# Moving the norm and rotation of attention heads onto VectorE alone and turning them two products later, in PSUM banks of their own

## The reference, cut to what matters

```python
q = apply_rope(rms_norm(q.reshape(B, S, 2 * H, D), q_gain), cos, sin)   # D = 64, 2 * H = 16
def rms_norm(x, gain):
    y = xf * lax.rsqrt(jnp.mean(xf * xf, axis=-1, keepdims=True) + EPS)
    return y * gain
def apply_rope(x, cos, sin):
    return concatenate([x1 * c - x2 * s, x2 * c + x1 * s], axis=-1)
```

## Time and profile before

| what | value |
|---|---|
| median of 3 runs | 2499.97 us (2494.35 to 2503.65) |
| profiled execution, its own time | 2496.57 us |
| its span | 2494.7 us |
| granted clock of TensorE, mean | 0.96 |
| busy: PE, PEld, DVE, ACT, POOL | 91%, 77%, 61%, 48%, 13% |

### The profile page before, as it was taken

One profiled execution on the slowest core, in us unless ns is written; L12 is line 12 of the kernel. 1 busy time (PEld: TensorE's weight loads), 2 busy tenths in 40 slices (PEclk: granted clock), 3 DMA queues, 4 the chain that ended last, 5 costly groups with the idle time before them and its releaser, 6 DMA issues.

```text
span 2494.7 us, 29578 instructions
## 1 busy us (share of the span) xinstructions
PE 2279.3 (91%) x11690; PEld 1917.5 (77%) x11690; DVE 1525.2 (61%) x2036; ACT 1203.5 (48%) x1829; POOL 313.7 (13%) x238
## 2 busy tenths in 40 slices
PE   6999999787998899999999999859999777899999
PEld 6877888776887668888877887738887566688887
DVE  5645656576656366557636666676655776554655
ACT  4555545446444445445555445444445344444543
POOL 0001000631000001000002000211000433154000
PEclk9999999899999999999999999969999898989999
DMA  6535565213564315565545655405565444401563
GB/s 215 184 132 163 185 200 167 78 51 121 190 199 148 114 68 180 194 194 169 169 135 160 205 185 165 157 17 150 184 202 170 119 136 121 152 1 52 172 199 118
DMA packets 200504, 369.32 MB, mean 148 GB/s; under 512 B 6863, under 2 KB 142415, under 8 KB 200368
## 3 DMA queue, kind: packets, MB, share of 16 engines
q1 hardware_dynamic: 196752, 358.70, 44.3%
q0 software_dynamic: 3616, 8.74, 1.9%
HBM read 366.36 MB, written 1.05 MB: 147 GB/s over the span
## 4 chain that ended last, share of the span: by engine, by line
PE 82%; DVE 11%; ACT 5%; issue 2%; DMA 1%; SPq 0%; DVEq 0%; POOL 0%; ACTq 0%
PE PS L641 42%; PE PS L758 13%; PE PS L755 6%; PE PS L742 5%; DVE wlo L1729 2%; PE PS L911 2%; PE PS L775 2%; PE PS L1192 1%; PE PS L776 1%; DVE U L1752 1%; ACT whi L1248 1%; PE PS L1160 1%; PE PS L833 1%; PE PS L1061 1%; ACT U L1268 1%
## 5 line engine op out<-in xcount | busy, mean ns | idle before, releaser
L1729 DVE TENSOR_TENSOR wlo<-raw,whi 128x1024 fp32r<-128x1024 f32 x658 | 808.5, 1252 | 265.7 <-ACT whi L1248 264.8
L1248 ACT ACTIVATE whi<-raw 128x1024 fp32r<-128x1024 f32 x680 | 700.2, 1056 | 364.8 <-PE PS L641 309.9
L641 PE MATMUL PS<-whi,U 128*128 128x512 f32 x1792 | 505.3, 399 | 23.6 <-DVE U L1752 7.5
L758 PE MATMUL PS<-U,whi 128*128 128x512 f32 x1440 | 507.4, 397 | 0.0
L641 PEld LDWEIGHTS PS<-whi,U 128*128 128x128 f32 x1792 | 338.7, 191 | 100.7 <-issue 26.5
L755 PE MATMUL PS<-U,wlo 128*128 128x256 f32 x1260 | 353.5, 281 | 0.0
L758 PEld LDWEIGHTS PS<-U,whi 128*128 128x128 f32 x1440 | 264.4, 188 | 51.9
L641 PE MATMUL PS<-wlo,U 128*128 128x512 f32 x896 | 279.8, 394 | 0.0
L641 PE MATMUL PS<-whi,fH 128*128 128x512 f32 x832 | 258.2, 391 | 0.9 <-DVE fL L1977 0.9
L1854 DVE TENSOR_TENSOR AR<-PS,AR 128x512 f32<-128x512 f32 x96 | 66.4, 691 | 314.3 <-ACT AR L1331 314.3
L641 PE MATMUL PS<-wlo,fH 128*128 128x512 f32 x832 | 256.3, 389 | 0.0
(11 more groups left out here) (298 smaller groups left out, 2615.6 us busy)
## 6 DMA issues: line engine op xcount, KB each, us to landing
raw<-in_mlp_w_up SPq DMA_DIRECT2D x64, 1024.0 KB, 5.5
raw<-in_mlp_w_down SPq DMA_DIRECT2D x64, 1024.0 KB, 5.0
raw<-in_ret_w_in SPq DMA_DIRECT2D x48, 1024.0 KB, 5.2
raw<-in_m_w_up SPq DMA_DIRECT2D x32, 1024.0 KB, 5.5
raw<-in_m_w_down SPq DMA_DIRECT2D x32, 1024.0 KB, 4.9
raw<-in_kv_w SPq DMA_DIRECT2D x24, 1024.0 KB, 5.2
raw<-in_ret_w_out SPq DMA_DIRECT2D x16, 1024.0 KB, 4.9
raw<-in_gla_w_in SPq DMA_DIRECT2D x12, 1024.0 KB, 5.1
```

Of the source, the lines that this page charges most:

```text
L641: mm = e.matmul(bank(b + nb), a, w[:, nb * 512:(nb + 1) * 512], start=(begins and n < 2), stop=(ends and n >= 4))
L758: mm = e.matmul(o, w_h[:, k, :], U[:, k, :, :, :], start=(k == 0), stop=(k == 7))
L1248: e.activation(split_half(whi, i, x), a, ACT.Copy).then_inc(HI.tick((i, x)), 1)
L1729: e.tensor_tensor(split_half(wlo, i, x), a, split_half(whi, i, x).bitcast(F32), ALU.subtract).then_inc(LO.tick((i, x)), 1)
```

## The change

1. DVE does the whole norm and rotation, upper and lower rows, in one function `head_work`. Its eight weight splits for one product (2 halves of 4 chunks) are placed between its pieces. POOL keeps only the DMAs of the gains.
2. ACT copies both halves of a product out of PSUM as soon as it is done (`head_read`), and squares the copy in SBUF later (`head_squares`). `qs` and `xs` are doubled; the second ones lie in parts of `v` that are not written yet.
3. All products of DIL and DIFF use banks 0 to 3. Product n + 1 waits for HCP (or LV, the copy of a v product) of product n. All products after the first of a stage also take the quarters of tt = 0 first in their first chunk.
4. Heads are turned into banks 4 to 7. In DIL the heads of product m are turned inside product m + 2, after its first chunk (after the second for m = 1). In DIFF the first heads are turned after the second chunk of product 2, and the second heads after product 2, as before.
5. The rows for "kv" are turned inside product 2 after its third chunk. ACT and DVE write the first half of them to `U` at the end of product 2 and the other half at the start of product 3.
6. In the attention part of DIL the scores stand in banks 4 to 6, the turned probabilities in 0 to 2, the values in 3 and 7. The first scores no longer wait for the last v copies (LV).

```diff
@@ PE
-            def turn_heads(key, qs, banks, free):
+            def turn_heads(key, qs, free):
...
-                                e.wait_ge(*(HPOOL[key] if tt == 0 else HDVE[key]))
+                                e.wait_ge(*HROT[key + (tt,)])
...
             def pe_diff(S):
-                gemm_a((S, 1), c0 + 4, 8, u_ap, (4, 6))
-                k0, k1 = (S, 0), (S, 1)
-                turn_heads(k0, p.qs[0], (0, 1, 2, 3), [[HSQ[k0 + (0,)]], [], [HSQ[k0 + (1,)]], []])
-                gemm_a((S, 2), c0 + 8, 8, u_ap, (0, 2), free=([HTC[k0 + (1,)]], [HTC[k0 + (3,)]]))
-                turn_heads(k1, p.qs[1], (4, 5, 6, 7), [[HSQ[k1 + (0,)]], [], [HSQ[k1 + (1,)]], []])
+                gemm_a((S, 1), c0 + 4, 8, u_ap, (0, 2), free=([HCP[k0 + (0,)]], [HCP[k0 + (1,)]]), entry=lambda: None)
+
+                def v_product(c):
+                    if c == 1:
+                        turn_heads(k0, p.qs[0], [[]] * 4)
+
+                gemm_a((S, 2), c0 + 8, 8, u_ap, (0, 2), free=([HCP[k1 + (0,)]], [HCP[k1 + (1,)]]), after=v_product,
+                       entry=lambda: None)
+                turn_heads(k1, p.qs[1], [[HTC[k0 + (j,)]] for j in range(4)])
...
             def pe_dil(S):
+                def beside(n, c):
+
+                    m = n - 2
+                    if 0 <= m < 6 and c == (1 if m == 1 else 0):
...
+                        turn_heads((S, m), p.qs[m % 2], free)
+                    if (n, c) == (2, 2):
+                        turn_kv()
 
                 for n in range(9):
...
-                    gemm_a((S, n), c0 + 4 * n, 8, u_ap, bs, fresh=fresh_u(t) if n in (0, 3) else None, free=free_for(n),
-                           entry={0: lambda: turn_in(S, 1), 3: lambda: None}.get(n))
-                    if 1 <= n <= 6:
-                        o = bs_of[(n - 1) % 2]
-                        f0, f1 = read_out(n - 1)
-                        turn_heads((S, n - 1), p.qs, (o[0], o[0] + 1, o[1], o[1] + 1), [f0, [], f1, []])
+                    gemm_a((S, n), c0 + 4 * n, 8, u_ap, (0, 2), fresh=fresh_u(t) if n in (0, 3) else None,
+                           free=read_out(n - 1) if n else ((), ()), after=lambda c: beside(n, c),
+                           entry=(lambda: None) if n else (lambda: turn_in(S, 1)))
@@ ACT
             def act_dil(S):
...
                     if n:
                         hi_of(c0 + 4 * n, 1)
+                        if n == 3:
+                            e.wait_ge(*USED[c0 + 11, 1])
+                            for tt in range(2):
+                                u_hi((S, "kv"), tt, 1, IN_KV)
                         if m < 6:
...
+                            head_squares((S, m), p.qs[m % 2], p.xs[m % 2])
+                        hi_of(c0 + 4 * n + 1, 1)
+                        if m < 6:
                             root((S, m), st[:, 64:96])
...
+                        if 2 <= n < 8:
+                            turn_heads((S, n - 2), p.qT[n - 2] if n < 5 else p.kT[n - 5])
+                        hi_of(c0 + 4 * n + 2, 2)
+                        if n == 2:
+                            e.wait_ge(*USED[c0 + 9, 1])
+                            for tt in range(2):
+                                u_hi((S, "kv"), tt, 0, IN_KV)
+                    if n < 6:
+                        head_read((S, n), p.qs[n % 2])
@@ DVE
+            def head_work(key, qs, xs, tab, i):
+
+                lo_of(i, 1)
+                if key == (DIL, 2):
+                    for tt in range(2):
+                        u_lo_in((DIL, "kv"), tt, 1, IN_KV)
+                head_sum(key, 0, xs)
+                head_sum(key, 1, xs)
+                head_mean(key)
+                lo_of(i + 1, 1)
+                head_root(key)
+                head_scale(qs, 0)
+                head_scale(qs, 1)
+                head_swap(qs, xs, tab, 0)
+                lo_of(i + 2, 1)
+                head_swap(qs, xs, tab, 1)
+                head_sum_of_both(key, qs, xs, tab, 0)
+                lo_of(i + 3, 1)
+                head_sum_of_both(key, qs, xs, tab, 1)
@@ POOL
-                for n in range(6):
-                    head_rotate((S, n), p.qs, p.xs, p.tab)
-                    if n < 5:
-                        e.wait_ge(*HTAB[S, n])
+                for n in range(5):
+                    e.wait_ge(*HTAB[S, n])
...
```

More of the change, by code:

```diff
@@ L258, in program @@
                 turns.append((S, "kv"))
-        turned = [(t, tt, j) for t in turns for tt in range(2) for j in range(2)]
+        turned = []
+        for t in turns:
+            turned += [(t, tt, j) for tt in range(2) for j in range(2)] if t[1] != "kv" else \
+                      [(t, tt, j) for j in range(2) for tt in range(2)]
         TURN = Event(sem("s_u_turned"), turned)
@@ new lines, in turn_kv @@
+                def turn_kv():
+                    e.wait_ge(*HTC[S, 0, 3])
+                    for j in range(2):
+                        for tt in range(2):
+                            turn_quarter((S, "kv"), tt, j, h)
+                def beside(n, c):
+                    m = n - 2
+                    if 0 <= m < 6 and c == (1 if m == 1 else 0):
+                        if m == 0:
+                            free = [[]] * 4
+                        elif m == 1:
+                            free = [[UL[(S, "kv"), j // 2, j % 2]] for j in range(4)]
+                        else:
+                            free = [[HTC[S, m - 1, j]] for j in range(4)]
+                        turn_heads((S, m), p.qs[m % 2], free)
+                    if (n, c) == (2, 2):
+                        turn_kv()
@@ L1260, in prime, with u_hi @@
                 e.activation(st[:, 200:201], ones[:, 0:1], ACT.Sqrt)
[L1262 to L1269, removed]
+            def u_hi(t, tt, j, gain):
+                e.wait_ge(*TURN[t, tt, j])
+                for kk in range(4):
+                    k, o = 4 * j + kk, (4 + 2 * tt + j) * 512 + kk * 128
+                    ins = e.activation(U[:, k, tt, 0, :], PS[:, o:o + 128], ACT.Copy, scale=gT[:, gain, k:k + 1])
+                ins.then_inc(UH.tick((t, tt, j)), 1)
             def u_hi_o(S):
@@ L1279, in next_in @@
             def next_in(S, tt):
-                u_hi_in((S, "in"), tt, S)
+                for j in range(2):
+                    u_hi((S, "in"), tt, j, S)
             def squares(S):
@@ L1658, in act_dil @@
+                        hi_of(c0 + 4 * n + 2, 2)
+                        if n == 2:
+                            e.wait_ge(*USED[c0 + 9, 1])
+                            for tt in range(2):
+                                u_hi((S, "kv"), tt, 0, IN_KV)
+                    if n < 6:
+                        head_read((S, n), p.qs[n % 2])
+                    else:
                         for tt in range(2):
                             e.wait_ge(*rows_done((S, n), tt))
-                            e.activation(p.v[n - 6][:, tt, :], bank(bs[tt], 2), ACT.Copy,
+                            e.activation(p.v[n - 6][:, tt, :], bank(2 * tt, 2), ACT.Copy,
@@ L2571, in pool_diff @@
                 seam(S - 1)
-                for n in range(2):
-                    head_rotate((S, n), p.qs[n], xn, p.tabs[n])
             def pool_dil(S):
```

201 lines of the change are left out of this document (66 added, 135 removed).

## The result

The changed kernel takes 2406.07 us (median of 4 runs, 2403.36 to 2408.56) against 2500.09 us before (4 runs, 2494.35 to 2503.65): a ratio of 0.9626, 95% interval 0.9605 to 0.9647, so 88 to 99 us less. Forecast were 2413 us and a gain of 85 us from one profiled execution to the other. The profiled executions took 2496.57 and 2405.15 us, 91.4 apart.

The account below looks back on a forecast made before the run. PE was taken as the bound, losing time in waits before turns of heads. Gains 67.4 + 1.3 - 2 + 18.5 = 85 us take the profiled 2496.57 to 2411.6, stated as 2413 for the median; range 2402 to 2434 (0.81).

Parts of the forecast that it names:

- The wait before the turns is what was lost, and it goes: PE's waits for POOL and DVE before turns of heads in DIL and DIFF fall from 69.0 us to some 2.
- The clock: PE's granted clock in DIL's products becomes 1.00 throughout; after stalls it ran at 0.51.
- DVE without GpSimd at 1.22 and 0.65: DVE's rotation without POOL computing: a scale takes 1.22 us, a half-width multiplication 0.65, the lower end of 0.65 to 1.22.
- slow rotation: Rival, chance 0.03: DVE's scale and half-width multiplications keep 2.31 and 2.71 us because of access patterns; load 33.5, time near 2490.
- the slower one: Rival, chance 0.04: table multiplications and sums on DVE also take 2.31 us; load 37.7, time 2522, range 2510 to 2540.
- DVE's load fits under the product: DVE's work per product is 23.1 us, within the 23.9 of a product with its turns.
- the margin before the turns: Rotated heads are ready on DVE at 24.7 us and wanted by PE at 29.3, counted from the preceding product's end.
- One set of banks costs nothing: ACT's copies free the banks in time between products; without cover, 1.1 to 2.7 us at each of ten hand-overs.
- 67.4 + 1.3 - 2: DIL's gain in us: turns 67.4, first scores not waiting for ACT's v copy 1.3, less 2 charged for kv rows.
- 18.5: DIFF's gain up to the first scores in us: 12.2 - 2.1 + 7.0 + 1.4, with 1.6 of wait left at the second heads.
- The last step of the prediction: From 2411.6 us for the profiled execution to 2413, with the median of runs 3.4 above the profiled execution.
- theory A: In the experiments' expectations, VectorE's queue order is the cause; GpSimd back gives 2406 to 2418 (turns late) or 2423 (early).

## Why the prediction was right, point by point

**The wait before the turns is what was lost, and it goes: right.** 69.0 us became 0.5.

**The clock: right.** The stretches of DIL and DIFF are granted 0.99 and 1.00 instead of 0.89 and 0.91. I had said 1.00 throughout; DIL's first product began at the low level.

**DVE without GpSimd at 1.22 and 0.65: right.** Measured 1.24 for a scale, 0.69 for a half-width multiplication, 0.60 to 0.62 from one start to the next. The rival "slow rotation" falls with it, and so does the slower one.

**DVE's load fits under the product: right, and by less than it seemed.** 22.4 against 23.56 us; the 1.17 between them is the wait for ACT's split, and one more instruction costs most of its length. DVE was busy 94.5 and 93.9% of the two rounds from 1980.31 us on, where I had said over 95. The working left out that the margin before the turns does nothing for the splits and for the kv rows, which the same queue delivers.

**One set of banks costs nothing: right.** No copy holds a matmul in the profile after, nor in the one profiled execution with doubled copies. In the run with the kv rows between the products one copy did, for 2.11 us, so the cover is there only while ACT's queue is free.

**The sum: 85 forecast, 91.4 between the profiled executions.** DIL was put at 67.4 + 1.3 - 2 = 66.7 and gave 68.5. A round is 1.80 and not 2.10 us above the product (seven times 0.3 is 2.1), and the kv rows cost 0.5 and not 2. Against it the first product of DIL now began at the low clock: its first sixteen matmuls took 5.34 us, 3.74 before. DIFF was put at 18.5 and gave 21.3: the second heads wait 0.5 and not 1.6, the turns are 0.3 cheaper, and its first sixteen matmuls took 3.73 us, at the high clock, where they took 5.31 before. These two shifts of 1.6 us stand in stretches ahead of any head, nothing in the change is known to cause them, and that they cancel is luck. The medians lie 94.0 apart, and their interval, 88 to 99, holds the 91.4. The last step of the prediction doesn't add up: 2411.6 and 3.4 are 2415, not 2413.

**What the prediction did not see is which part does it.** It priced the two functions of the change, less load and later turn, as if one hid the rest. The runs give, step by step, from 2497 us with only banks and buffers:

| step | us | gain |
|---|---|---|
| banks, buffers, kv rows alone | 2497.0 | 2 to 3, no difference that can be measured |
| + sums, root and rotation between the splits (queues of DVE and ACT) | 2456.7 | 40 |
| + turns two products later | 2432.3 | 24 |
| + GpSimd out, VectorE alone | 2406.1 | 26 |

The last two in the other order: VectorE alone 42 (2456.7 to 2414.6), turns later 8.5. And VectorE alone in the kernel before, with its old order, banks and buffers: 14. So no part is worth a fixed amount. My theory A in the expectations, that order alone is the cause and the rest is small, fell with the two runs in which GpSimd is back: it was 20 and 34 us off in them, and 21 in the one with the rotation behind the last split.

What fits all runs that changed the load is this: after the change of order, time goes by DVE's load against 23.56 us, and load comes from instructions and from contention alike. In DIL, DVE's busy time grows by 7.25, 15.12, 22.13 and 42.76 us and the stretch by 4.15, 16.34, 20.40 and 36.50 (one more instruction, GpSimd back, three more, GpSimd's additions). What fits less well is my forecast of the size. Contention and three more instructions cost more than the load alone, and the reason is visible in PE's busy time. DIL's stretch with GpSimd back (late turns):

```profile
1890.69:2118.50 227.81, 216.82 (x974) 177.89 (x972) 183.27 (x164) 125.24 (x160) 84.04 (x45) 0.96 0.56 168
```

And with three more instructions:

```profile
1891.03:2122.90 231.87, 216.34 (x974) 177.49 (x972) 190.28 (x212) 125.56 (x160) 7.99 (x15) 0.96 0.56 165
```

Against the changed kernel's 211.47 and 208.90, the first is 16.3 us longer, of which 7.9 are busy time of the same matmuls, the second 20.4, of which 7.4. So 48 and 36% of the loss in DIL is matmuls that run longer, at a granted clock of 0.96 instead of 0.99, and not waiting. In my forecasts for these runs I counted the waits alone.

Open: how far copies could be delayed before they hold PE was tried at one step only, without a verdict. How ACT's part of the new order and DVE's share the 40 us was not tried.

## What to carry to other kernels

When two engines share a job and both read SBUF with two-input instructions, count the job on one of them alone before believing that sharing helps: here GpSimd needed 12.4 us for half the rows and VectorE beside it 10.3 for the other half, and VectorE alone needs 10.1 for all. Put a side job between the feeding instructions of its queue, not behind them, and compute the load of that queue per period first: a late deadline hides latency, never load. Look for every other result that the same queue owes: here the splits and the kv rows were late where the turns were not. And read PE's busy time in a stretch beside its idle time, since the stalls here cost again in clock.

## What the runs showed of the hardware that was not expected

- 70.9 us of GpSimd's additions on scratch lengthened DVE's busy time by 42.8 us, with no data in common: 1.4 to 1.5 us for each DVE instruction beside them, half-width (0.68 to 2.05 and 2.16) or full.
- DVE's busy time in DIL fell (187.22 to 168.15 us) when it took over GpSimd's half of the work.
- Sixteen fp32 turns of 128 x 128 inside a run of matmuls delay them by 1.67 us; between a stall and a product at the low clock, 3.56.
- In the run with GpSimd back and late turns, a few stalls in DIL (four for DVE's splits, 2.0 us at most, and one of 3.0) go with a mean granted clock of 0.96 over 228 us, and with 7.9 us more busy time for the same matmuls.
